# First block's output projection: rounded three-part products in place of exact ones, two loads and two small steps elsewhere

## The reference

```
y_m  = sigmoid(o) * (normed heads)        # 4 heads of 128
y_p  = pooled, mixed and scaled           # 4 groups of 128
x    = x + concat([y_m, y_p]) @ w_out     # 1024 x 1024: the output projection
h    = rmsnorm(x, norm2_g)
x    = x + moe_ffn(h, ...)                # 32 experts, 4 to a token
x    = rmsnorm(x, normf_g)
x    = second_block(x, ...)               # projections, two kinds of attention, FFN
```

## Time and profile before

| | |
|---|---|
| median of 3 runs | 1613.13 us (1611.69 to 1614.2) |
| profiled execution, its own time | 1614.05 us |
| its span | 1612.3 us |
| mean granted TensorE clock | 0.996 |
| PE busy | 1564.9 us, 97% |
| PEld busy | 882.2 us, 55% |
| DVE busy | 629.7 us, 39% |
| ACT busy | 499.2 us, 31% |
| POOL busy | 291.2 us, 18% |
| DMA, over the span | 507.67 MB, mean 315 GB/s |

### The profile page before, as it was taken

How to read it: one execution, slowest core, us unless ns; L and a number is a source line. 1 busy time by engine, 2 the same in 40 slices (tenths; PEclk the granted TensorE clock), 3 DMA queues, 4 the chain that set the end, 5 groups by cost and what they waited for, 6 DMA issues and landing times. The chain is left out here.

```text
span 1612.3 us, 21430 instructions
## 1 busy us (share of the span) xinstructions
PE 1564.9 (97%) x8406; PEld 882.2 (55%) x8406; DVE 629.7 (39%) x1177; ACT 499.2 (31%) x795; POOL 291.2 (18%) x179
## 2 busy tenths in 40 slices
PE   9999999999999999999999999999999999999998
PEld 8843333333333333323233233588899888888886
DVE  7742212121212212112121121396476456658752
ACT  6431111111111111111101111366556553467753
POOL 2600000000000000000000000274333323435552
PEclk9999999999999999999999999999999999999999
DMA  9699999999999999999999999644234234556552
GB/s 349 233 380 354 427 427 427 427 427 426 428 426 428 427 428 426 427 428 428 428 428 428 428 428 427 248 157 157 78 115 144 84 105 162 205 167 212 180 187 104
DMA packets 94889, 507.67 MB, mean 315 GB/s; under 512 B 10059, under 2 KB 35448, under 8 KB 70104
## 3 DMA queue, kind: packets, MB, share of 16 engines
q1 hardware_dynamic: 94568, 505.97, 77.8%
q10 hardware_dynamic: 240, 0.55, 0.1%
HBM read 505.46 MB, written 1.05 MB: 314 GB/s over the span
## 5 line engine op out<-in xcount | busy, mean ns | idle before, releaser
L190 POOL TENSOR_TENSOR low<-ring,high 128x1024 fp32r<-128x1024 f32 x81 | 201.7, 2491 | 1261.9 <-ACT high L187 1261.8
L1741 PE MATMUL ps<-ring,x 128*64 128x512 f32 x1536 | 341.9, 595 | 20.9 <-DMA ring<-in_w_up 20.9
L1741 PEld LDWEIGHTS ps<-ring,x 128*64 128x64 f32 x1536 | 106.0, 137 | 252.7 <-issue 207.0
L187 ACT CAST high<-ring 128x1024 fp32r<-128x1024 f32 x162 | 168.0, 1052 | 110.0 <-PE ps L1993 28.4
L1782 PE MATMUL ps<-ring,x 128*64 128x512 f32 x752 | 172.0, 600 | 1.2 <-issue 0.8
L190 DVE TENSOR_TENSOR low<-ring,high 128x1024 fp32r<-128x1024 f32 x81 | 107.4, 1326 | 95.0 <-ACT high L187 94.3
L1584 DVE TENSOR_SCALAR hT<-ps 128x512 f32<-128x512 f32 x32 | 22.1, 692 | 291.7 <-PE ps L1741 291.7
L1741 PE MATMUL ps<-extra,x 128*64 128x512 f32 x512 | 114.6, 595 | 5.8 <-DMA extra<-in_w_up 5.8
L1958 PE MATMUL ps<-hTb,high 128*128 128x512 f32 x464 | 116.4, 393 | 0.5 <-PEq L2917 0.5
L1782 PEld LDWEIGHTS ps<-ring,x 128*64 128x64 f32 x752 | 52.5, 138 | 100.7 <-issue 100.0
L1651 ACT COPY gpickT<-ps 128x256 f32<-128x256 f32 x32 | 11.9, 373 | 282.1 <-PE ps L1761 282.1
(11 more groups left out here) (518 smaller groups left out, 2302.8 us busy)
## 6 DMA issues: line engine op xcount, KB each, us to landing
ring<-in_w_down SPq DMA_DIRECT2D x52, 2048.0 KB, 32.7
ring<-in_w_gate SPq DMA_DIRECT2D x48, 2048.0 KB, 31.2
ring<-in_w_up SPq DMA_DIRECT2D x47, 2048.0 KB, 31.1
ring<-in_w_in SPq DMA_DIRECT2D x22, 2048.0 KB, 7.9
extra<-in_w_gate SPq DMA_DIRECT2D x16, 2048.0 KB, 31.4
extra<-in_w_up SPq DMA_DIRECT2D x16, 2048.0 KB, 29.7
extra<-in_w_down SPq DMA_DIRECT2D x14, 2048.0 KB, 34.5
ring<-in_w_up SPq DMA_DIRECT2D x24, 1024.0 KB, 7.2
```

What stands on the lines that cost most here:

```text
L187: eng.copy(hi, self.raw(u)).then_inc(self.sem("high_split"), 1)
L190: eng.tensor_tensor(lo, self.raw(u), hi.bitcast(F32), ALU.subtract).then_inc(self.sem(who + "_split"), 1)
L1741: last = pe.matmul(bank[h * CAP:(h + 1) * CAP, :], xg[:, c, kh, :], w[:, c, h * 512:(h + 1) * 512], start=False, stop=kh == 1 and c == 3)
```

## The change

Five edits.

1. The 32 exact products of the output projection become 96 rounded ones. w_out is split as eight further units, 20 to 27, of 256 rows by 512 columns: u20, u21 (n = 0) and u22, u23 (n = 1) are the pooled half; u24, u26 (n = 0) and u25, u27 (n = 1) the heads'. POOL makes the low parts of 22 to 25, DVE of the others. ACT evacuates y rounded (`yTh`), DVE makes the rest (`yTl`, `rows_low`). These two lie where `spare[0]` is.
2. PE's order: the n = 0 pooled units, then those of n = 1; the transposes of the heads stand between the high and the low products of u23. Then u24, u25, the biases, and u26 and u27 by token tile.
3. SP's order: the loads of `btab` and of piece 95 move from behind bank ("o", 1) to behind ("out", 1, 1).
4. At the end of phase A, `row_half` comes after both additions of a token tile, `row_scale` of tile 0 after all four.
5. In phase C, hg = 0, the two subtractions of `row_low` move behind the first half of the third convolution.

```diff
-    BY_ONE = (4, 6, 8, 10, 12)
+    BY_ONE = (4, 6, 8, 10, 12, 22, 23, 24, 25)
+    FIRST_OUT = 20
...
+            yTh_first, yTl_first = (sb(w, [P, KC, S], F32R, first) for w in ("yTh_first", "yTl_first"))
...
+    for n, q, key in ((0, 2, None), (0, 3, None), (1, 2, None), (1, 3, None), (0, 0, None), (1, 0, None),
+                      (0, 1, ("out", 0, 1)), (1, 1, ("out", 1, 1))):
+        splits.units.append((OUT0 + n, "rows", q, key))
...
-            for n, use in ((0, ("qk", 3)), (1, ("u", 1)), (2, ("v", 1)), (3, ("o", 1)), (Pieces.LATE[2], ("o", 1)), (Pieces.LATE[1], ("pool", 1)),
-                           (6, ("ym", 1)), (7, ("ym", 1)), (4, ("out", 0, 1)), (5, ("out", 1, 1)), (Pieces.LATE[0], ("out", 1, 1))):
+            for n, use in ((0, ("qk", 3)), (1, ("u", 1)), (2, ("v", 1)), (3, ("o", 1)), (Pieces.LATE[1], ("pool", 1)),
+                           (6, ("ym", 1)), (7, ("ym", 1)), (4, ("out", 0, 1)), (5, ("out", 1, 1)),
+                           (Pieces.LATE[0], ("out", 1, 1)), (Pieces.LATE[2], ("out", 1, 1))):
                 banks.done(sp, use)
-                if n == Pieces.LATE[2]:
+                if n == Pieces.LATE[0]:
...
-            splits.ahead(act, "high", 20)
+            splits.ahead(act, "high", 23)
...
             k.prepare(act)
+            splits.ahead(act, "high", 24)
             act.wait_ge(sem("hvar"), 1)
             act.activation(rs[:, :], rs[:, :], ACT.Sqrt).then_inc(sem("hroot"), 1)
+            splits.ahead(act, "high", 26)
+            for c in range(4):
+                bank = banks.take(act, ("ym", c // 2))
+                act.activation(yTh[:, c, :], bank[:, (c % 2) * S:(c % 2 + 1) * S], ACT.Copy,
+                               scale=prm1[:, P1["head_norm_g"] + c:P1["head_norm_g"] + c + 1]).then_inc(sem("y_high"), 1)
+            splits.ahead(act, "high", 28)
...
+            def rows_low(c, key, gain):
+                bank = banks.take(v, key)
+                v.wait_ge(sem("y_high"), (c + 4) % KC // 2 * 2 + 2)
+                last = v.scalar_tensor_tensor(yTl[:, c, :], bank[:, (c % 2) * S:(c % 2 + 1) * S], prm1[:, gain:gain + 1],
+                                              yTh[:, c, :].bitcast(F32), ALU.mult, ALU.subtract)
...
-                    if n == 0:
-                        k.row_half(v, "n2", 1, t, EPS1)
-                if t == 0:
-                    k.row_scale(v, chain, "n2", 1, t, by_row_of_four)
+                k.row_half(v, "n2", 1, t, EPS1)
+            k.row_scale(v, chain, "n2", 1, 0, by_row_of_four)
...
+            def out_units(us, highs, rows_from, begin=False, between=None):
+                for i, u in enumerate(us):
+                    splits.high_ready(pe, u)
+                    pe.wait_ge(sem("y_high"), highs[i])
+                    for t in range(NT):
+                        out_products(u, t, yTh, splits.hi, begin=begin and i == 0)
+                    if between and i == 1:
+                        between()
+                    splits.ready(pe, u)
+                    for t in range(NT):
+                        out_products(u, t, yTh, splits.lo)
+                for i, u in enumerate(us):
+                    banks.moved(pe, rows_from[i])
+                    for t in range(NT):
+                        last = out_products(u, t, yTl, splits.hi)
+                    splits.finish(last, u)
...
                 if hg == 0:
+                    conv(2, "gv", hg, (0,))
                     v.wait_ge(sem("row_high"), 2)
...
-                conv(2, "gv", hg)
+                    conv(2, "gv", hg, (1,))
```

More of the change, by code:

```diff
@@ L731, in phase_a @@
     vext = part(0, KC * S, NT, NH, P + 1, of=spare)
+    yTh, yTl = env["yTh_first"], env["yTl_first"]
     og = part(1, 12 * S, NT, W)
@@ L976, in _ @@
             g.tensor_tensor(inv[:, :, :], inv[:, :, :], uT[:, :, :], ALU.subtract).then_inc(sem("pooled"), 1)
+            splits.ahead(g, "low1", len(splits.units))
         @block.vector
@@ L1117, in _ @@
                     .then_inc(sem("ym"), 1)
[L1118 to L1122, removed]
+            for c in range(4):
+                rows_low(c, ("ym", c // 2), P1["head_norm_g"] + c)
+            splits.ahead(v, "low0", 28)
             bank = banks.take(v, "prm2")
@@ L1330, in _ @@
             outs = {}
[L1331 to L1341, removed]
@@ L1342, in _ @@
-            pooled_half(0, 1)
-            pooled_half(1, 0)
-            pe.wait_ge(sem("ym"), NT)
-            for j in range(2):
-                bank = banks.claim(pe, ("ym", j))
-                for i in range(2):
-                    for t in range(NT):
-                        c = 2 * j + i
-                        last = pe.transpose(bank[:, i * S + t * P:i * S + (t + 1) * P], og[:, t, c * P:(c + 1) * P],
-                                            ident[:, :])
-                banks.filled(last, ("ym", j))
@@ L1353, in _, with out_products, heads_transposed @@
-            pooled_half(1, 1)
+            def out_products(u, t, rows, weights, begin=False, end=False):
+                g, _, q, _ = splits.units[u]
+                for i in range(2):
+                    last = pe.matmul(outs[g - OUT0, t], rows[:, 2 * q + i, t * P:(t + 1) * P], weights(u)[:, i, :],
+                                     start=begin and i == 0, stop=end and i == 1)
+                return last
+            def heads_transposed():
+                pe.wait_ge(sem("ym"), NT)
+                for j in range(2):
+                    bank = banks.claim(pe, ("ym", j))
+                    for i in range(2):
+                        for t in range(NT):
+                            c = 2 * j + i
+                            last = pe.transpose(bank[:, i * S + t * P:i * S + (t + 1) * P], og[:, t, c * P:(c + 1) * P],
+                                                ident[:, :])
+                    banks.filled(last, ("ym", j))
@@ L1354, in _ @@
+            for n in range(2):
+                for t in range(NT):
+                    outs[n, t] = banks.claim(pe, ("out", n, t))
+                out_units([Splits.FIRST_OUT + 2 * n + i for i in range(2)], (2, 4), (("pool", 0), ("pool", 1)), True,
+                          heads_transposed if n else None)
+            for n in range(2):
+                out_units([Splits.FIRST_OUT + 4 + n], (6,), (("ym", 0),))
             pe.wait_ge(sem("prow2_in"), 16 * 5)
@@ L1356, in _ @@
             banks.filled(pe.transpose(bank[:, 0:113], prow2[0:113, :], ident[0:113, 0:113]), "prm2")
-            for j in range(2):
-                banks.moved(pe, ("ym", j))
             def raw_transposes(n, t):
@@ L1368, in raw_transposes @@
                         banks.filled(last, ("n2", j))
+            pe.wait_ge(sem("y_high"), KC)
+            banks.moved(pe, ("ym", 1))
             for t in range(NT):
                 for n in range(2):
+                    u = Splits.FIRST_OUT + 6 + n
                     if n == t == 1:
                         raw_transposes(0, 0)
-                    for c in range(4):
-                        last = pe.matmul(outs[n, t], yT[:, c, t * P:(t + 1) * P], piece(OUT0 + n)[:, c, :],
-                                         start=False, stop=c == 3)
-                    banks.filled(last, ("out", n, t))
+                    splits.high_ready(pe, u)
+                    out_products(u, t, yTh, splits.hi)
+                    out_products(u, t, yTl, splits.hi)
+                    splits.ready(pe, u)
+                    last = out_products(u, t, yTh, splits.lo, end=True)
+                    if t == 0:
+                        banks.filled(last, ("out", n, 0))
+                    else:
+                        splits.finish(last, u)
             raw_transposes(0, 1)
```

20 lines of the change are left out of this document (12 added, 8 removed).

## The result

The changed kernel takes 1616.3 us (median of 16 runs, 1614.61 to 1617.25), the kernel before 1613.44 us (16 runs, 1611.16 to 1614.91): ratio 1.002, 95% interval 1.0014 to 1.0027, so 2.9 us slower. The forecast was 1613.8, its range 1608 to 1618. The profiled execution of the changed kernel took 1617.25 us with a span of 1615.4, 3.1 more than the span before; its trace can be read against the old one directly.

The account below looks back on a forecast made before the run. The experts were taken to be bound by their weight stream, so a later start at the front moves the end. Front and stream +4.4, phase C −3.7, sum +0.7: 1613.13 becomes 1613.8 us, range 1608.0 to 1618.0.

Parts of the forecast that it names:

- Part A: Output projection: POOL's two low parts block DVE's head scalings, PE waits 5.8 us, out(1,1) full at 114.0, +3.4.
- Rival 1: Output projection: POOL does not block the scalings, heads ready at 91.2, total 1608.1 us; chance 0.17.
- rival 2: Output projection: only POOL's first low part delays the scalings, heads ready at 93.3, total 1611.5 us; chance 0.13.
- Part B, the tail: End of phase A: tile 0's scaling now precedes the evacuation the router awaits, +1.4; first expert starts 4.8 us later.
- Part B, the stream: Experts' weight stream: the late loads and late first expert delay it by +4.4, between +3.9 and +4.8.
- by bytes +3.9: Weight stream: next piece starts 5.9 us later behind the late loads; 2.0 us of old queue gaps are made good.
- by PE's freeing of slots +4.8: Weight stream: ring slots that PE frees start the transfers, so the first expert's 4.8 us delay is paid in full.
- The five loads: Behind out(0,1): pieces 4, 5, 47, 95 and btab, 8.8 MB, keep the queue 20.5 us, from 112.1 to 132.6.
- Part C: Phase C: the earlier gate-row low part removes PE's 3.0 us wait and 1.7 of half clock, less 1; net −3.7.
- Rival 3: Phase C: unit 12's low part loses the ports to POOL twice, PE waits as before, total 1617.5 us; chance 0.15.
- "same": Whole kernel: time within 0.2% of the kernel before, neither below 1609.9 nor above 1616.4 us; chance 0.55.
- "slower": Whole kernel: time above 1616.4 us, over 0.2% slower than the kernel before; chance 0.20.

Follow-up runs that it names:

- e3: Changed kernel, but POOL waits for the heads' products before making the low parts of units 23 to 25; 1612.58 us, ratio 0.9997 to the kernel before.
- e5: Changed kernel with DVE's old order of row_half and row_scale at the end of phase A; 1616.28 us, ratio 1.0021 to the kernel before.
- e7: Kernel before, with only the loads of btab and piece 95 moved behind out(1,1); 1615.23 us, ratio 1.0013 to the kernel before.
- e8: Changed kernel, with pieces 4 and 5 issued as soon as w_out's raw halves are split; 1614.13 us, ratio 1.0004 to the kernel before.
- e1: Kernel before, with only the gate rows' two low-part subtractions moved behind the first half of the third convolution; 1609.84 us, ratio 0.9979.
- e2: Changed kernel with the gate rows' two subtractions back in their old place; 1619.64 us, ratio 1.0041 to the kernel before.
- e4: Changed kernel, but DVE makes the low parts of units 23 and 24 behind the heads' products; 1610.37 us, ratio 0.9984 to the kernel before.
- e9: Changed kernel, with units 23 and 24's low parts on DVE and pieces 4 and 5 issued once w_out is split; 1608.09 us, ratio 0.9963.

## Why the prediction was right or wrong, point by point

- **Part A: right, nearly to the number.** Heads and transposes 95.6 foretold, 94.97 measured; PE's wait 5.8 against 5.2; the second wait 1.2 against 0.9; out(1,1) 114.0 against 114.08. That last agreement is in part luck: the transposes came 0.6 us earlier than foretold, and the stretch from there to the end of the second wait ran 2.3 us longer than its sum at the upper level, where 1.5 was put. The blocking of the scalings by both of POOL's low parts, one scaling getting in between, is what the trace has, and e3 shows it to be the cause. Rival 1 (no blocking) and rival 2 (one low part paid) are out. Here the Trainium skill (SBUF — State Buffer, section "Who interferes with whom") holds for each single instruction: a scaling ends when POOL's ends. It does not say that the next scaling will lose again to POOL's next instruction; that came from row L2500 of the earlier trace rows, and it was worth 2.3 us. The row of L1072 said it more plainly than the prediction read it: not one of its four was slow but two, 1.11 and 1.39 us long, ending at 54.47 and 55.79 us, as POOL's two instructions at L960 ended at 54.32 and 55.64.
- **Part B, the tail: right against the kernel before, wrong as the price of the edit.** The evacuations came 2.0 us after out(1,1) instead of 0.6, the +1.4 foretold; 0.4 of it came back in the router's products, and the first expert was 4.4 late, not 4.8. But e5 shows that the old place would have been no better: between the faster rounded products there is no gap left for the scaling.
- **Part B, the stream: the step that failed.** The sentence was "by bytes +3.9, by PE's freeing of slots +4.8. I take +4.4 and keep both". Measured are 5.6 at the product before 1006 us and 6.3 at the experts' last. The bytes were the bound, and their end was mis-sized, 3.9 for 5.6 (5.9 at 160 us, 5.6 at 170). Both terms of it were off. The five loads kept the queue not for 20.5 us but for some 24.5, until about 137.7 us: 1.2 are the bytes of `gain`, which I had put at nothing; 1.1 were lost while btab ran, which I had charged only its 0.4 MB (283 and 326 GB/s from 124 to 128 us; 1.3 in e7's windows); 0.7 at the start, before the queue was full (287 GB/s from 114 to 116 us); about 1 I cannot assign. So the next piece came 10 us later than before, not 5.9. Against that the old queue's gaps, of which I credited 2.0 us, gave back some 4. And what I took for the upper end, PE's slots, bound nothing in the changed kernel: e8 gains 2.2 us with PE as late as ever. With it falls the sentence that whatever delays PE before about 160 us is paid in full; that holds only while the queue is not full.
- **Part C: right in kind, a little smaller.** −3.7 foretold, −3.0 to −3.3 measured (e1, e2). The 3.0 us wait and the half clock behind it went. The new wait at the squares came at 0.7 us (1 foretold), and a second one of 0.7 at L2825, which the forecast did not have, makes the difference. Rival 3, the low part losing the ports twice, did not come: DVE's was 1.72 us long in place of 1.23, and done in time.
- **The sum:** +0.7 foretold, +2.9 measured: 1.2 to 1.9 from the stream, 0.4 to 0.7 from phase C. The measured time lies in the range, and between the forecast and rival 3 in size, with another cause than rival 3's; "same" had 0.55 and "slower" 0.20, and the result lies just at the border of the two.

## What to carry to other kernels

Where a long stretch is bound by its stream, cost an edit at the front in bytes not yet moved at the moment when the queue becomes full for good, and not in the start of the consumer: e4 had out(1,1) 2.0 us before the kernel before, and no more bytes moved; e8 had PE as late as the changed kernel, and 3.0 us more of bytes moved by 170 us. When operands are split into parts, the raw copy is free as soon as the parts are made; let the next load wait for that and not for the product (about 2 us here). And work that is given to POOL because it is idle should not run while DVE is on the critical path: two instructions of POOL made 2.14 us of DVE into 6.02 here. Put off until the heads were done (e3) they gave back 3.7 us, taken over by DVE behind its own products (e4) 5.9.

## What the runs showed of the hardware that I had not expected

A small table of 0.4 MB in three DMAs costs a full queue some 1.3 us beyond its bytes: 307 and 266 GB/s in two windows where the queue otherwise moves 426 and 434, the DMA engines being as busy. The same dip stands in the same two windows of e4 (285 and 297) and e8 (250 and 260), where btab is late too. The Trainium skill (SBUF — State Buffer, section "Door 1: The DMA port swizzle (why `[64,N]` ≈ `[32,N]`)") says that a transfer into 32 partitions, as each of btab's three is, reaches only half of the ports and some 218 GB/s; by it my estimate for 0.39 MB is 1.8 us in place of 0.9, 0.9 us lost, which agrees with most of the 1.1 to 1.3 measured. No run here loads the table in another layout.

And in the kernel before, 16 records of products that follow two short waits at 139 to 142.6 us take 5.31 us, the clock being 0.51 there; in the changed kernel, behind the same two waits 4.4 us later, they take 3.65 (the second row is a window, columns as in the earlier trace rows):

```profile
142.58 5.31 PE L1782 MATMUL ps<-ring,x 128*64 128x512 f32 x16 [0.83 <-issue]
...
144.00:146.00 2.00, 2.00 (x7) 0.53 (x4) 0.00 (x0) 0.00 (x0) 0.00 (x0) 0.51 1.09 467
```

```profile
146.95 3.65 PE L1830 MATMUL ps<-ring,x 128*64 128x512 f32 x16 [0.83 <-issue]
```

So of the first expert's 4.4 us PE was only 2.7 late at 150 us, by nothing that the edits aimed at. Of the 13 traces four have the slow form (the kernel before, e1, e3 and e9) and nine the other. Which it is to be, I cannot tell from these runs. In the changed kernel it did not count, since the queue was full there; the kernel before still had gaps in its queue at that time (387 GB/s from 130 to 160 us), so there it may have cost something, which no run separates.
